# A second place for past keys, a later state fetch, and value products mixed with gate tiles in a two-layer hybrid decoder step

## What is computed

```python
(q, kc, vc, ks, vs, kw, vw, g_nsa, u, o_pre, if_pre, g_a, g_b) = split_cols(h @ w_in)
# A: sparse attention: compressed, selected and window branches, 8 query heads, 2 key heads
o_nsa = g[..., 0:1] * o_cmp + g[..., 1:2] * o_sel + g[..., 2:3] * o_win
# B: mLSTM matrix memory: conv, block-diagonal q/k/v, state C (8 x 4 x 128 x 128 for the samples)
num = (s * dw) @ v + w_inter * (q @ c0)
merged = sigmoid(g_a) * (o_nsa @ w_up_a) + sigmoid(g_b) * (o_m @ w_up_b)
x = x + merged @ w_out
x = x + channel_mixer(rmsnorm(x))     # layer 0: dense SwiGLU; layer 1: top-2 of 8 experts
```

## Time and profile before

| | |
|---|---|
| median of 3 runs | 1853.33 us (1851.79 to 1854.4) |
| the profiled execution's own time | 1854.55 us |
| its span, first to last instruction | 1852.9 us |
| mean granted TensorE clock | 0.963 |
| TensorE busy (matmul) | 1746.0 us, 94% |
| VectorE, ScalarE, GpSimd busy | 1035.3, 810.8, 176.7 us |

### The profile page before, as it was taken

The page is one execution under the profiler, slowest core; times in us unless marked ns, Lnnn a source line. Parts: engine busy times, 40 slices in busy tenths (PEclk is TensorE's granted clock), DMA queues, the critical chain, the costliest instruction groups (busy, mean ns, idle before and its releaser), DMA issues.

```text
span 1852.9 us, 22952 instructions
## 1 busy us (share of the span) xinstructions
PE 1746.0 (94%) x8548; PEld 1394.4 (75%) x8548; DVE 1035.3 (56%) x1189; ACT 810.8 (44%) x873; POOL 176.7 (10%) x237
## 2 busy tenths in 40 slices
PE   6999979997999989998999899999999999999997
PEld 4567667777999956766776578888888888888875
DVE  2043421615454212343143468888888888888887
ACT  2013331114343110333120357777777767676764
POOL 2222011210000042201121010000000000000020
PEclk9999988998999989999899789999999999999999
DMA  8348323172554455521416389999999999999993
GB/s 239 122 156 253 112 67 93 52 229 63 165 180 163 90 163 183 159 69 58 103 46 214 134 301 332 401 351 400 356 402 350 400 352 403 352 395 360 393 391 122
DMA packets 230152, 424.92 MB, mean 229 GB/s; under 512 B 32414, under 2 KB 127934, under 8 KB 229884
## 3 DMA queue, kind: packets, MB, share of 16 engines
q1 hardware_dynamic: 217244, 383.62, 59.2%
q0 software_dynamic: 12832, 40.28, 6.6%
HBM read 403.70 MB, written 24.29 MB: 231 GB/s over the span
## 4 chain that ended last, share of the span: by engine, by line
PE 85%; DVE 6%; DMA 4%; ACT 2%; issue 2%; DVEq 0%; POOLq 0%; POOL 0%; SPq 0%; ACTq 0%
PE ps L717 81%; PE ps L721 4%; DMA weights_in<-in_moe_w 2%; DVE weights_low L1725 2%; DVE arena L1725 2%; ACT weights_high L1343 1%; DMA out_s_conv<-arena 1%; DVE arena L1912 1%; DMA arena<-in_cache_win 0%; DVE arena L1739 0%; DMA arena<-in_vecs 0%; POOLq L2415 0%; DMA arena<-in_state_conv 0%; DVE arena L1742 0%; DVE ffn_low L1725 0%
## 5 line engine op out<-in xcount | busy, mean ns | idle before, releaser
L717 PE MATMUL ps<-arena 128*128 128x288 f32 (+20 forms) x3180 | 719.9, 384 | 32.9 <-DMA arena<-in_vecs 8.9
L717 PEld LDWEIGHTS ps<-arena 128*128 128x128 f32 (+7 forms) x3180 | 508.9, 183 | 224.6 <-issue 91.5
L1725 DVE TENSOR_TENSOR weights_low<-weights_in,weights_high 128x3072 fp32r<-128x3072 f32 (+1 forms) x192 | 589.2, 3088 | 108.6 <-ACT weights_high L1343 108.4
L1343 ACT ACTIVATE weights_high<-weights_in 128x3072 fp32r<-128x3072 f32 (+1 forms) x192 | 489.6, 2560 | 200.2 <-PE ps L717 173.0
L717 PE MATMUL ps<-weights_high,item_high 128*128 128x512 f32 x704 | 279.2, 397 | 7.9 <-DVE weights_low L1725 7.2
L717 PE MATMUL ps<-weights_low,item_high 128*128 128x512 f32 x704 | 275.5, 391 | 0.0
L717 PE MATMUL ps<-weights_high,item_low 128*128 128x512 f32 x704 | 275.5, 391 | 0.0
L1340 ACT ACTIVATE arena<-arena 128x128 f32<-128x128 f32 (+12 forms) x188 | 74.9, 413 | 290.6 <-DVE arena L1725 95.8
L717 PEld LDWEIGHTS ps<-weights_high,item_high 128*128 128x128 f32 x704 | 133.3, 189 | 37.0 <-DVE weights_low L1725 9.6
L1343 ACT ACTIVATE arena<-ps 128x512 f32<-128x512 f32 (+16 forms) x146 | 63.3, 463 | 211.3 <-PE ps L721 136.6
L717 PEld LDWEIGHTS ps<-weights_high,item_low 128*128 128x128 f32 x704 | 133.1, 189 | 28.2
(11 more groups left out here) (182 smaller groups left out, 1438.1 us busy)
## 6 DMA issues: line engine op xcount, KB each, us to landing
weights_in<-in_moe_w SPq DMA_DIRECT2D x192, 768.0 KB, 8.1
weights_in<-in_moe_w SPq DMA_DIRECT2D x48, 1536.0 KB, 9.5
weights_in<-in_moe_w SPq DMA_DIRECT2D x64, 512.0 KB, 5.0
ffn_in<-in_ffn_w SPq DMA_DIRECT2D x30, 1024.0 KB, 7.1
weights_in<-in_moe_w SPq DMA_DIRECT2D x16, 1024.0 KB, 9.0
arena<-in_w_in SPq DMA_DIRECT2D x32, 384.0 KB, 4.0
arena<-in_w_in SPq DMA_DIRECT2D x32, 256.0 KB, 5.0
token_slots<-arena SPq DMA_DIRECT2D x12, 512.0 KB, 6.3
```

Source lines behind the costliest of these rows:

```text
L717: return nc.tensor.matmul(out, lhsT, rhs, start=start, stop=stop)
L1343: return nc.scalar.activation(out, x, ACT.Copy, scale=scale)
L1725: return V.tensor_tensor(out, x, y, op)
```

## The change

The second half's keys get a place of their own in area Y (over `kvT2`, which is dead after `hid_pe`), and their nine fetches are issued directly behind `hid_pe`. The state C, which lies in Y too, is fetched after the last transpose of keys_turned(1). The second half's values are fetched as before, behind `spv_pe` of the first half. On TensorE `sample_values` takes a gate tile with it: after each pair of value matmuls comes one of the tile's eight matmuls. The first half takes tile 12, the second takes tile 15 (in PSUM bank 5, for which it waits for VectorE's second token product, `ktk_ev`); probs_turned(1) comes directly behind the first block, then tiles 13 and 14. ScalarE's order follows: gate_tanh(15) moves behind the copies of the token projections.

```diff
-        swK, swV = (take(2048, at)... for at in (X_at, X_at + 2560))
+        swV = take(2048, X_at + 2560).rearrange("p (r b g c) -> p r b g c", r=2, b=4, g=2)
+        swK = [take(2048, at).rearrange("p (r b g c) -> p r b g c", r=2, b=4, g=2) for at in (X_at, Y_at)]
...
-                def sample_values(t, bank):
+                def sample_values(t, bank, gate, gate_bank):
...
                             for g in range(2):
                                 mm(ps[:, bank, 32 * b:32 * b + 32], swV[:, r, b, g, :], PTs[:, r, g, 32 * b:32 * b + 32],
                                    False, False)
+                            gate_part(gate, gate_bank, 2 * b + r)
...
+                def gate_part(n, bank, k):
+
+                    x, d = GATE_TILES[n]
+                    sem, at, w = in_of(f"G{n // 2}", l)
+                    if k == 0:
+                        pe.wait_ge(sem, at)
+                        pe.wait_ge(gt_ev.sem, gt_ev.at(l, n - 1))
+                    m = mm(ps[:, bank, 0:N], w[:, k, (d % 2) * P:(d % 2) * P + P], hT[:, k, :], k == 0, k == KD - 1)
+                    if k == KD - 1:
+                        m.then_inc(gt_pe.sem, 1)
...
-                pe.wait_ge(sw_in.sem, sw_in.at(l, 160))
+                pe.wait_ge(sw_in.sem, sw_in.at(l, 304))
                 pe.wait_ge(gt_ev.sem, gt_ev.at(l, 10))
                 pe.wait_ge(sa_ev.sem, sa_ev.at(l))
                 keys_turned(0)
...
                 sample_scores(0)
-                pe.wait_ge(sw_in.sem, sw_in.at(l, 304))
                 keys_turned(1)
...
                 probs_turned(0)
-                gate_tile(12, 0)
-                sample_values(0, 4)
+                sample_values(0, 4, 12, 0)
+                probs_turned(1)
                 gate_tile(13, 1)
-                probs_turned(1)
                 gate_tile(14, 0)
-                gate_tile(15, 1)
...
                 pe.wait_ge(sw_in.sem, sw_in.at(l))
-                sample_values(1, 7)
+                pe.wait_ge(ktk_ev.sem, ktk_ev.at(l, 2))
+                sample_values(1, 7, 15, 5)
...
                 pe.wait_ge(ktk_ev.sem, ktk_ev.at(l))
+                pe.wait_ge(gt_ev.sem, gt_ev.at(l))
                 up_a(0)
...
                 pool.wait_ge(hid_pe.sem, hid_pe.at(l))
-                pool.dma_start(C0[:, :, :, 0:MD].rearrange("p b h e -> p (b h) e"),
-                               a["state_C"][l].rearrange("b h d e -> d (b h) e")).then_inc(c0_in.sem, 16)
+                second_four(swK[1], 0)
                 pool.wait_ge(mqk_ev.sem, mqk_ev.at(l))
...
-                for dst, o, freed in ((swK, 0, skt_pe.at(l, 4)), (swV, P, spv_pe.at(l, 1))):
-                    pool.wait_ge((skt_pe if o == 0 else spv_pe).sem, freed)
-                    for b in range(4, 8):
-                        for g in range(2):
-                            pool.dma_start(dst[:, 0, b - 4, g, :], page(l, "cache_slc", b, g)[:, o:o + P]).then_inc(sw_in.sem, 16)
-                    window(dst, 1, o)
+                pool.wait_ge(skt_pe.sem, skt_pe.at(l))
+                pool.dma_start(C0[:, :, :, 0:MD].rearrange("p b h e -> p (b h) e"),
+                               a["state_C"][l].rearrange("b h d e -> d (b h) e")).then_inc(c0_in.sem, 16)
+                pool.wait_ge(spv_pe.sem, spv_pe.at(l, 1))
+                second_four(swV, P)
```

More of the change, by code:

```diff
@@ L224, in build @@
         cmpN = take(9 * 512, X_at).rearrange("p (s c) -> p s c", s=9)
-        swK, swV = (take(2048, at).rearrange("p (r b g c) -> p r b g c", r=2, b=4, g=2) for at in (X_at, X_at + 2560))
+        swV = take(2048, X_at + 2560).rearrange("p (r b g c) -> p r b g c", r=2, b=4, g=2)
         mk = take(3 * 512, X_at).rearrange("p (m h e) -> p m h e", m=3, h=MH)
@@ L959, in keys_turned @@
                         r, b, g = i // 8, (i // 2) % 4, i % 2
-                        m = tr(ps[:, 2 + i // 4, (i % 4) * P:(i % 4) * P + P], swK[:, r, b, g, :])
+                        m = tr(ps[:, 2 + i // 4, (i % 4) * P:(i % 4) * P + P], swK[t][:, r, b, g, :])
                         if i % 4 == 3:
@@ L1036, in _ @@
                     if kind == 0:
-                        pe.wait_ge(gt_ev.sem, gt_ev.at(l))
+                        pe.wait_ge(gt_ev.sem, gt_ev.at(l, 15))
                     for m in range(3):
@@ L1472, in _ @@
                 gate_tanh(12, 0)
+                probs_turned(1)
                 gate_tanh(13, 1)
-                probs_turned(1)
                 gate_tanh(14, 0)
-                gate_tanh(15, 1)
                 act.wait_ge(rt_pe.sem, rt_pe.at(l))
@@ L1486, in _ @@
                     copy(dst, ps[0:n, VB[0][m], :].rearrange("p (h e) -> p h e", h=MH)).then_inc(vt_ev.sem, 1)
+                gate_tanh(15, 5)
                 def decayed(h):
@@ L2465, in _, with second_four @@
                         src = page(l, "cache_slc", b, g)
-                        x, y = swK[:, 0, b, g, :], swV[:, 0, b, g, :]
+                        x, y = swK[0][:, 0, b, g, :], swV[:, 0, b, g, :]
                         dst = bass.AP(x.tensor, x.offset, [x.ap[0], [y.offset - x.offset, 2], x.ap[1]])
                         pool.dma_start(dst, src.rearrange("p (u c) -> p u c", u=2)).then_inc(sw_in.sem, 16)
-                window(swK, 0, 0)
+                window(swK[0], 0, 0)
                 window(swV, 0, P)
+                def second_four(dst, o):
+                    for b in range(4, 8):
+                        for g in range(2):
+                            pool.dma_start(dst[:, 0, b - 4, g, :], page(l, "cache_slc", b, g)[:, o:o + P]).then_inc(sw_in.sem, 16)
+                    window(dst, 1, o)
                 pool.wait_ge(hid_pe.sem, hid_pe.at(l))
-                pool.dma_start(C0[:, :, :, 0:MD].rearrange("p b h e -> p (b h) e"),
-                               a["state_C"][l].rearrange("b h d e -> d (b h) e")).then_inc(c0_in.sem, 16)
+                second_four(swK[1], 0)
                 pool.wait_ge(mqk_ev.sem, mqk_ev.at(l))
```

## The result

The changed kernel took 1828.33 us (median of 4 runs, 1821.91 to 1830.27), the kernel before 1853.87 us on the same chip (4 runs, 1851.79 to 1854.52): a ratio of 0.9858, 95% interval 0.9831 to 0.9886. Forecast 1824, range 1819 to 1837. The profiled execution took 1826.45 us, its span is 1824.8.

What follows compares the result with a forecast made beforehand. TensorE, 85% of the span, was held by 17.9 us of waits for window keys and a low clock. The stretch shrinks to 48.95 us from 64.72 and 63.41, saving 30.2 us: 1824 us, range 1819 to 1837.

Steps and rivals of the forecast that it cites:

- rival (a): At gates(0): the clock falls there all the same, as in both layers before; +3.8 us, 1828 us; chance 0.13.
- The keys' own place: Ahead of keys_turned(1): standstills of 8.57 and 9.12 us go wholly, and the transposes drop from 3.67 to 1.97 us.
- The lost cover of gate 12: Ahead of sample_values(0): three ScalarE copies, formerly under gate 12, become a new standstill of 1.25 us per layer.
- The size of the mixed block: In each mixed block: value products plus gate tile cost their sum, 4.81 + 3.97 = 8.78 us; bounds 8.0 and 9.2.
- rival f: In the mixed blocks: the mix hides loads, four blocks 1 to 2 us shorter, 1816 to 1820 us; chance 0.04.
- I take it that it stays: In the mixed blocks: the clock stays up, at 1.00 throughout, so each block takes 8.78 us.
- rival (c): In mixed blocks: clock falls after 3.6 us for 7.1 us, 3.55 us lost per block; 1842 us; chance 0.10.
- rival (d): In the mixed blocks: the mix counts as value products and all runs at 1.2 GHz, 1863 us; chance 0.02.
- rival (e): Ahead of the first mixed block: turns and new wait let the clock fall, 3.5 us per layer, 1831 us; chance 0.03.
- gates(0) at 2.4 GHz: From sample_out to gates(1): at full clock 5.5 us in place of 7.42 and 7.50, 1.9 us back per layer.
- Rival (b): Ahead of the second values: their fetch lands late, 1 to 2.5 us per layer at worst, 1825 to 1829 us; chance 0.10.
- (g): Near the second keys: their wait hid another of like size, so the gain fails; about 1840 us; chance 0.02.

Runs made afterwards that it cites:

- keys_only: Kernel before with only the second keys' own place, their early fetch and the late state_C; TensorE's order unchanged: 1830.16 us, ratio 0.9865.
- mix_only: Changed kernel with one swK again, refilled behind keys_turned(0), and state_C fetched behind hid_pe: 1849.92 us, ratio 0.9961.
- wait_double: Changed kernel with two more ScalarE copies, read by nobody, ahead of the three that sample_values(0) waits for: 1835.74 us, ratio 0.9888.
- shift: Changed kernel with gate tile 12 whole ahead of sample_values(0), which mixes tile 13 instead; tile 14 alone follows probs_turned(1): 1841.62 us, ratio 0.9936.
- unmixed: Changed kernel with each gate tile's eight matmuls in one run between past values and new rows, not interleaved: 1827.92 us, ratio 0.9855.
- the changed kernel again: The changed kernel, nothing altered, measured and profiled a second time: 1831.10 us, ratio 0.9859; stages 66.58 and 55.92 us.
- head13_early: Changed kernel with tile 13's first three matmuls ahead of sample_values(0)'s ScalarE wait and gates(0) ahead of the second mixed block: 1827.87 us, ratio 0.9832.
- head_early: Changed kernel with tile 12's first three matmuls ahead of sample_values(0)'s ScalarE wait and gates(0) ahead of the second mixed block: 1817.47 us, ratio 0.9803.
- early_gates: Changed kernel with gates(0) ahead of the second mixed block, whose values go to PSUM bank 4: 1819.48 us, ratio 0.9818.
- head13: Changed kernel with tile 13's first three matmuls ahead of sample_values(0)'s ScalarE wait, its other five behind probs_turned(1): 1823.20 us, ratio 0.9836.
- head_early again: The head_early kernel, nothing altered, measured a second time on another chip: 1826.58 us, ratio 0.9826; stages 53.98 and 58.87 us.

## Why the prediction was right, and where it was off

The time lay within the range and 4 us above the forecast; it is rival (a)'s time, 1828 us, and (a) is what the first profile shows. Step by step, for layer 0 (predicted, measured in the windows above; layer 1 took 50.97 in all):

| step | predicted | measured |
|---|---|---|
| second keys, gate 11, scores and turns, new wait | 1.97 + 3.97 + 2.59 + 1.25 = 9.78 | 9.71 |
| first mixed block | 8.78 | 8.77 |
| probabilities to token projections | 16.11 | 15.95 |
| second mixed block | 8.78 | 8.71 |
| sample_out, gates(0) to gates(1) | 5.5 | 0.76 + 7.03 = 7.79 |
| sum | 48.95 | 50.93 |

- **The keys' own place** did what the forecast says. The standstill went, 16.34 to 7.47 us and 16.85 to 7.46 us from the first keys' start to the second's: 18.3 us of the 26.8. The transposes behind it went from 3.67 to 1.95 us in each layer, 3.4 us more. keys_only, whose stages are 23.2 us shorter than before (21 expected), shows that this part alone makes the gain.
- **State_C later** cost nothing and mqz's delay neither: in the list of waits nobody waits for either. The estimate of 25 us for its transfer was twice too long (12.6 us), which changes nothing.
- **The lost cover of gate 12**: 1.10 us on TensorE (1.37 on its weight loads) against 1.25. Right.
- **The size of the mixed block** as the sum of its parts was right to 0.1 us: no hidden loads (rival f), no price for the changes of kind.
- **"I take it that it stays"** is the step that failed, though the first profile seems to bear it out. The clock stayed up in three of the four first blocks that the changed kernel's two profiles show, and in one it stayed down from 1.7 us to its end (6.5 us lost in the block, 8.2 with the steps behind). The four second blocks all stayed up. That the first profile shows no fall is therefore in part luck. Of rival (c) the price per block, 3.55 us, was too small: I took the clock to be back within 7.1 us, as in the values before (the rows give 6.8 us, for the clock was back near 289.5 and not 289.8). In this mix it wasn't: it stayed at 0.50 to the block's end in that block, in the first block of one layer each of mix_only and wait_double, and in both second blocks of shift (block records of 14.6 to 16.4 us). The reason given against rival (d), that the clock always came back during gate work before, doesn't hold behind layer 1's wait: there it came back during transposes, as rival (e) itself says. Against unmixed and keys_only the mix has gained nothing measurable.
- **gates(0) at 2.4 GHz** is the term that was mis-sized: 7.79 for 5.5 us in layer 0's rows above, and layer 1's stage is as long, which is rival (a): 26.4 us saved by it, 26.8 measured. At full clock the step takes 0.75 + 4.55 = 5.3 us (unmixed, both layers; the changed kernel again, layer 1), so its size was right and its clock was not certain. The reason given, a denser block ahead, doesn't decide it: behind second blocks that all ran at 1.00 the changed kernel's stretch from gates(0) fell in three layers of four.
- **Rival (b)**: no wait in the changed kernel. The second values' window fetch is issued 10.2 us behind the first block in it, as predicted. Where TensorE came earlier, its first reader was held until 4.6 to 6.0 us behind that issue (shift 292.13 to 296.86; head13_early 884.96 to 890.99), and the changed kernel's reader comes at 5.7 us: the reserve is about 1 us or none, where the forecast had 0.5. The Trainium skill's fit ("DMA: Bandwidth & Descriptors", Anatomy of one DMA), by estimate 3.2 us, is too short for this fetch; the runs decide.
- **Rivals (e) and (g)** didn't come: the turns and the new wait ahead of the first block stand at 1.00 in both layers of both profiles of the changed kernel, and no new wait of like size took the place of the keys' wait.
- A slip without effect: a page costs GpSimd 1.11 us, as the division says, not 1.14; the sum goes on with 9 us for eight.

What is left open: what decides in which execution the clock falls. The Trainium skill ("TensorE: Matmul & The Clock Gate", Part 1) says that the chip judges TensorE's activity on a schedule of its own that doesn't start with the kernel, and that counts of slow matmuls differ from run to run. The repeats agree with that; none of these runs tests it.

**A version that beats both.** Both runs of head_early lie below the changed kernel's two: 0.9803 and 0.9826 against 0.9858 and 0.9859, some 8 us, which is what the two stages say (2 x 4.4 us). Its first interval lies clear of the changed kernel's, its repeat's overlaps them, and so does that of early_gates (0.9818), which by its stages (55.15 us) gives most of it. Only some 1.9 us a layer of this is order and cover (53.98 against 55.92 us, the changed kernel again in layer 1, where the clock fell nowhere); the rest is clock.

## What to carry to other kernels

A place of its own for data that is otherwise fetched behind its predecessor's last reader is worth the wait and the slow work behind it; price both, and then look at the next fetch of the same kind, since an order that reaches it 1.5 to 4 us sooner (head13, shift) brought a wait back, and in head13_early a whole block at half clock behind a wait of 1.5 us. Put a product whose result feeds a chain on other engines (here gates(0)) ahead of independent matmuls rather than behind them: at full clock this gave 0.8 us a layer. With it the stretch up to gates(1) stayed at 1.00 in seven of eight layers, against seven of eighteen in the nine profiles that have gates(0) behind the block (the kernel before not counted); whether the order is the reason isn't shown. And profile the same program twice before a clock trace is taken as the kernel's own: one profile of the changed kernel would have "shown" that the mix keeps the clock up.

## What the runs showed of the hardware

- Once at 1.2 GHz, a block of small value products interleaved with gate matmuls didn't bring the clock back while it lasted (block records of 14.6 to 16.4 us, all busy), whereas it was back at the end of 3.67 us of nothing but transposes, and the clock was back within a whole gate tile (unmixed, near 273.9).
- The clock can fall in a busy TensorE without any standstill ahead: in head_early again 45.62 us are all busy, with a mean clock of 0.89.
- Executions of one program differ by up to 15 us of 1830 (mix_only 1842.6 to 1857.6, wait_double 1828.4 to 1843.1, the changed kernel 1821.9 to 1835.6 over both its measurements), far more than the 3.7 us that I had taken as what a measurement can tell. Where two profiles of one program stand side by side, falls of the clock make the difference of their stages.
